# Six layer norms whose root is applied inside the transposition: a diagonal moving operand, beta as a small product, the rows in x_tok scaled a stage later

## The reference, cut to what matters

```python
def layer_norm_2(x, g, b):
    mu = jnp.mean(xf, axis=-1, keepdims=True)
    var = jnp.mean(jnp.square(xf - mu), axis=-1, keepdims=True)
    return ((xf - mu) * lax.rsqrt(var + LN_EPS) * g + b).astype(x.dtype)
...
x = layer_norm(ALPHA * x + recurrent(x), ...)        # norm 0
x = layer_norm(ALPHA * x + hier_moe(x), ...)         # norm 1
for l in range(2):                                   # second block
    x = layer_norm_2(ALPHA_2 * x + 0.5 * swiglu(x, ...), ...)   # norms 2, 5
    y = mlstm_mixer(x, ...) if l == 0 else window_attention(x, ...)
    x = layer_norm_2(ALPHA_2 * x + y, ...)                      # norms 3, 6
    x = layer_norm_2(ALPHA_2 * x + 0.5 * swiglu(x, ...), ...)   # norms 4, 7
```

## Time and profile before

| what | value |
|---|---|
| median of 3 runs | 1694.35 us (1694.08 to 1695.98) |
| the profiled execution's own time | 1697.26 us |
| its span | 1695.5 us, mean granted PE clock 0.976 |
| PE busy | 1592.3 us (94%), x9238 |
| DVE busy | 779.7 us (46%) |
| ACT busy | 505.8 us (30%) |
| POOL busy | 61.4 us (4%) |

### The profile page before, as it was taken

The page is one execution under the profiler, slowest core; times in us unless marked ns, Lnnn a source line. Parts: engine busy times, 40 slices in busy tenths (PEclk is TensorE's granted clock), DMA queues, the critical chain, the costliest instruction groups (busy, mean ns, idle before and its releaser), DMA issues.

```text
span 1695.5 us, 21971 instructions
## 1 busy us (share of the span) xinstructions
PE 1592.3 (94%) x9238; PEld 1172.1 (69%) x9238; DVE 779.7 (46%) x1028; ACT 505.8 (30%) x573; POOL 61.4 (4%) x104
## 2 busy tenths in 40 slices
PE   8997899999999998999998899999999997899997
PEld 7744433333333336999896689998999986689997
DVE  1584411111111116544656675456544566564445
ACT  1251100000000003334354234342443435433432
POOL 2000000000000000000000000000000000000000
PEclk9997899999999999999999999999999998999999
DMA  6705799999999999753223578554554221387500
GB/s 198 250 1 232 290 415 429 428 429 429 428 428 429 429 412 353 268 183 114 75 78 122 174 243 292 185 185 161 202 190 157 98 76 74 100 288 264 193 0 26
DMA packets 149457, 395.27 MB, mean 233 GB/s; under 512 B 9442, under 2 KB 109920, under 8 KB 136592
## 3 DMA queue, kind: packets, MB, share of 16 engines
q1 hardware_dynamic: 146656, 385.67, 60.5%
q0 software_dynamic: 2736, 8.68, 1.4%
HBM read 393.28 MB, written 1.05 MB: 233 GB/s over the span
## 4 chain that ended last, share of the span: by engine, by line
PE 67%; DMA 14%; DVE 10%; issue 3%; SPq 3%; ACT 2%; POOL 1%; POOLq 0%; DVEq 0%; ACTq 0%
PE bank L1355 29%; DMA ring<-in_moe_w_dram 14%; PE bank L1368 12%; PE bank L885 8%; PE bank L914 2%; PE bank L697 2%; SPq L267 2%; PE bank L1343 2%; PE bank L1575 1%; PE bank L902 1%; PE bank L644 1%; PE bank L1900 1%; PE bank L934 1%; DVE stats L539 1%; PE bank L683 1%
## 5 line engine op out<-in xcount | busy, mean ns | idle before, releaser
L885 PE MATMUL bank<-ring,arena 128*64 128x512 f32 x928 | 228.4, 596 | 9.5 <-DMA ring<-in_moe_w_dram 9.5
L1355 PE MATMUL bank<-x_hi,split_u_hi 128*128 128x256 f32 x688 | 194.9, 283 | 0.0
L1355 PE MATMUL bank<-x_hi,split_u_lo 128*128 128x256 f32 x688 | 194.7, 283 | 0.0
L1355 PE MATMUL bank<-x_lo,split_u_hi 128*128 128x256 f32 x688 | 194.7, 283 | 0.0
L1355 PE MATMUL bank<-x_lo,split_g_hi 128*128 128x256 f32 x656 | 185.6, 283 | 0.0
L1355 PE MATMUL bank<-x_hi,split_g_lo 128*128 128x256 f32 x656 | 185.6, 283 | 0.0
L1355 PE MATMUL bank<-x_hi,split_g_hi 128*128 128x256 f32 x656 | 185.6, 283 | 0.0
L885 PEld LDWEIGHTS bank<-ring,arena 128*64 128x64 f32 x928 | 69.3, 137 | 146.3 <-issue 114.7
L1265 DVE TENSOR_TENSOR split_g_lo<-ring,split_g_hi 128x2048 fp32r<-128x2048 f32 x47 | 107.7, 2292 | 127.7 <-ACT split_g_hi L1259 127.7
L1115 DVE SCALAR_TENSOR_TENSOR arena<-arena,work 128x256 f32<-128x256 f32 x32 | 15.5, 485 | 287.7 <-PE bank L934 287.7
L1265 DVE TENSOR_TENSOR split_u_lo<-ring,split_u_hi 128x2048 fp32r<-128x2048 f32 x45 | 103.1, 2292 | 69.0 <-ACT split_u_hi L1259 69.0
(11 more groups left out here) (352 smaller groups left out, 2504.8 us busy)
## 6 DMA issues: line engine op xcount, KB each, us to landing
ring<-in_moe_w_dram SPq DMA_DIRECT2D x92, 2048.0 KB, 19.1
ring<-in_ffn_w_in_dram SPq DMA_DIRECT2D x88, 1024.0 KB, 5.5
ring<-in_ffn_w_out_dram SPq DMA_DIRECT2D x44, 1024.0 KB, 5.5
ring<-in_ml_w_in_dram SPq DMA_DIRECT2D x12, 1024.0 KB, 5.2
ring<-in_rec_w_in_dram SPq DMA_DIRECT2D x10, 1024.0 KB, 11.6
ring<-in_at_w_in_dram SPq DMA_DIRECT2D x6, 1024.0 KB, 5.2
ring<-in_rec_w_out_dram SPq DMA_DIRECT2D x5, 1024.0 KB, 13.6
gb_row<-in_ln_g_dram POOLq DMA_DIRECT2D x8, 512.0 KB, 7.3
```

Source lines behind the costliest of these rows:

```text
L885: i = nc.tensor.matmul(bank[4 + p][64 * j:64 * j + 64, :], xe[p][:, k, :], unit_view(n, 4)[:, k % 4, :], start=(k == 0), stop=(k == KT - 1))
L1355: i = nc.tensor.matmul(up_bank(kind, s_)[:, m * T:(m + 1) * T], w, xp_[b][:, k, :], start=(k == 0 and j == 0), stop=(k == KT - 1 and j == 2))
```

## The change

In norms 1 to 6 the root no longer has to be in `x_tok` before PE starts. ACT builds `turn_diag`, the unit matrix times `rstd` on its rows; PE multiplies the centred tile with it, which transposes and scales at once. Beta comes into the same bank as a product ahead of it: `beta_r` (36 rows: the eight pieces of beta rounded, in rows 0 to 3, and the rest, in rows 32 to 35) with `blocks_r`, a constant matrix of ones in four blocks. `x_tok` itself is scaled later, in `finish_rows`, which the next stage calls. The rest of the diff merges the semaphores of the two attention-like stages (`ml["s"]`, `at["s"]` and others become `hd["s"]`, with counts moved by MLH) and places new tensors over dead ones; that is left out here.

```diff
+        def finish_rows(dve, L):
+            for t in range(TT):
+                for hf in range(2):
+                    dve.wait_ge(G["ln_tr"], 4 * L + 2 * t + hf + 1)
+                    scaled_rows(dve, L, t, hf)
...
         def norm_pool(pool, L):
...
+            if L in SPLIT_NORMS:
+                parts = bs.rearrange("o (b k p) -> (o k) b p", b=2, p=P)
+                pool.wait_ge(G["ln_blo"], 2)
+                for row in (0, 32):
+                    pool.dma_start(beta[row:row + 4], parts).then_inc(s_gbrow, 16)
...
         def norm_dve(dve, own, L, alpha):
...
+            if L in SPLIT_NORMS:
+                dve.wait_ge(s_gbrow, rows_loaded(L))
+                dve.wait_ge(G["ln_bhi"], SPLIT_NORMS.index(L) + 1)
+                nc.vector.tensor_tensor(beta_r[32:36], beta[32:36], beta_r[32:36].bitcast(F32), ALU.subtract).then_inc(G["ln_blo"], 1)
+                for t in range(TT):
+                    residual(t, 0)
+                    residual(t, 1)
+                    moments(t)
+                    centred(t, 0)
+                    centred(t, 1)
...
         def norm_evac_act(act, L):
+            if L in SPLIT_NORMS:
+                act.wait_ge(s_gbrow, rows_loaded(L))
+                act.wait_ge(G["ln_tr"], 4 * L)
+                nc.scalar.activation(beta_r[:], beta[:], ACT.Copy).then_inc(G["ln_bhi"], 1)
             for t in range(TT):
+                if L in SPLIT_NORMS:
+                    act.wait_ge(G["ln_rstd"], 2 * L + t + 1)
+                    nc.scalar.activation(turn_diag[:, t, :], ident[:], ACT.Copy, scale=rstd[:, t:t + 1]).then_inc(G["ln_diag"], 1)
...
         def norm_pe(pe, L):
             for t in range(TT):
                 keep_warm(pe, WARM[t])
+                n = SPLIT_NORMS.index(L) if L in SPLIT_NORMS else None
+                if n is not None:
+                    pe.wait_ge(G["ln_blo"], n + 3)
+                    pe.wait_ge(G["ln_cen"], 4 * n + 2 * t + 1)
+                    for b in range(2):
+                        nc.tensor.matmul(bank[4 + 2 * t + b][:], beta_r[:, b, :], blocks_r[:], start=True, stop=False,
+                                         skip_group_check=True)
+                    pe.wait_ge(G["ln_diag"], 2 * n + t + 1)
...
+                        i = nc.tensor.matmul(o, x_tok[:, t, k * P:(k + 1) * P], turn_diag[:, t, :], start=False, stop=(k % 4 == 3),
+                                             skip_group_check=True)
...
         moe_dve, ahead of expert 0:
+            own.did(nc.vector.memset(beta[:], 0.0))
+            own.then(nc.vector.tensor_scalar(rows, wide, 0.0, None, ALU.mult))
+            for row in (0, 32):
+                nc.vector.tensor_tensor(rows[row:row + 4], wide[0:4], ident[0:4, 0:4].unsqueeze(2).broadcast_to((4, 4, P)),
+                                        ALU.mult).then_inc(G["ln_blo"], 1)
...
         ffn_dve:
+                if s_ == 0:
+                    finish_rows(dve, NORM_AHEAD[f])
```

More of the change, by code:

```diff
@@ L127, in build @@
         ident = sb("ident", [P, P])
+        small_at = nc.sbuf_base
+        MS = sb("ml_small", [P, 256])
+        raw_at = nc.sbuf_base
+        misc_raw = sb("misc_raw", [8 * CH, P])
+        ng_raw = sb("ng_raw", [KT, P])
+        beta = nc.alloc_sbuf_tensor_at("beta", [36, 2, P], F32, offset=raw_at)
+        iota_at = nc.sbuf_base
+        iota_s = sb("iota_s", [P, SLOTS])
+        blocks_r = nc.alloc_sbuf_tensor_at("blocks_r", [36, HALF], F32R, offset=iota_at)
         upper = sb("upper", [P, P])
@@ L171, in build @@
         G = {}
-        for name in ("ln_in", "ln_var", "ln_rstd", "ln_half", "ln_tr", "ln_evac", "ln_lo"):
+        for name in ("ln_in", "ln_var", "ln_rstd", "ln_half", "ln_tr", "ln_evac", "ln_lo", "ln_cen", "ln_diag",
+                     "ln_bhi", "ln_blo"):
             G[name] = sem(name)
@@ L516, in pool_program, with rows_loaded @@
                     at_pool(pool)
+        def rows_loaded(L):
+            return 32 * (L + 1) + 32 * len([n for n in SPLIT_NORMS if n <= L])
         def norm_pool(pool, L):
@@ L558, in norm_dve @@
             if L > 0:
                 dve.wait_ge(G["ln_half"], 4 * L)
[L560 to L573, removed]
+            if L in SPLIT_NORMS:
[8 more added lines that the diff above has]
+                    centred(t, 1)
+            else:
+                residual(0, 0)
+                residual(0, 1)
+                moments(0)
+                dve.wait_ge(s_gbrow, rows_loaded(L))
+                centred(0, 0)
+                centred(0, 1)
+                scaled(0, 0)
+                scaled(0, 1)
+                residual(1, 0)
+                residual(1, 1)
+                moments(1)
+                for hf in range(2):
+                    centred(1, hf)
+                    scaled(1, hf)
@@ L1102, in moe_dve @@
             nc.vector.memset(h_e[0:64, :], 0.0).then_inc(mo["h0"], 1)
+            rows = blocks_r[:].rearrange("q (k j) -> q k j", k=4)
+            wide = ones[0:36, :].unsqueeze(1).broadcast_to((36, 4, P))
+            own.did(nc.vector.memset(beta[:], 0.0))
[3 more added lines that the diff above has]
+                                        ALU.mult).then_inc(G["ln_blo"], 1)
             for b in range(BLOCKS):
@@ L1641, in turned_weights @@
             def turned_weights(h):
[L1642 to L1643 removed]
+                act.wait_ge(hd["tr"], h + 1)
+                nc.scalar.activation(p_T[h % 2], bank[H_BANK[h]][:].rearrange("p (s j) -> p s j", s=TT), ACT.Copy).then_inc(hd["pt"], 1)
             def output_high(h):
```

111 lines of the change are left out of this document (60 added, 51 removed).

## The result

The changed kernel takes 1700.36 us (median of 9 runs, 1696.66 to 1701.69), the kernel before 1694.35 (9 runs, 1693.61 to 1696.33). The ratio is 1.0032, with a 95% interval of 1.0022 to 1.0042: it is slower, by more than the 0.2% that can be told. The forecast was 1692.1, with a range up to 1695.5.

A forecast was written before the change was run, and what follows sets the result against it. The prediction took norms to cost what PE loses between stages, waiting for DVE. Norms 2 to 6 (-0.4), norm 6's clock (-1.1) and norm 1 (-0.7) gave -2.2 us, from 1694.35 to 1692.1; range 1689.5 to 1695.5.

The forecast's parts named there:

- PE's own work is the bound of norms 2 to 6: Norms 2 to 6: the second diagonal is ready 0.9 us before PE wants it, so PE never waits.
- T: PE's first start in a norm, from which the forecast counted when the other engines' results are ready.
- Its sum, 6.3 us: PE's work per norm: beta 0.46 twice, diagonals 1.79 twice, warm products 1.79; norms 2 to 6 change by -0.4 us.
- that they have 36 rows instead of 128 should change nothing: Beta's products in each norm: priced like 512-column short-format products at 0.228 us, so 0.46 a pair.
- The clock no longer falls in norm 6: Norm 6: PE no longer waits, so the fall to the low clock level goes, saving 1.1 us.
- In norms 2 to 5, where PE waits less long: Reason given for norm 6's gain: with shorter waits in these norms the next products ran at full pace, 5.74 us.
- Norm 1: First norm: DVE waits 1.5 us for beta, yet -0.7 us in all; bounds -2.5 and +3.8.
- rise at 654.0: Norm 1: PE's clock falls at about 650.4, rises at 654.0 and doesn't fall a second time.
- 665.0: Norm 1: end of the next stage's 48 products in the kernel before, against 664.3 forecast for the changed one.
- What is hidden: Scalings (3.0 us of DVE), expert-stage DVE instructions (2.1 us) and beta's preparation in norms 2 to 6 lie under waits.
- Rival A: Low clock in norm 1 vanishes early, other stages' stretches move: -1.8 and -0.8 us more, 1689.5; chance 0.19.
- C: Diagonal products dearer than warm ones, +1.8 us a norm, 1702.9; decided by a fill from 7.3 us; chance 0.08.

The follow-up runs named there:

- beta_first: The changed kernel with all four beta products of a norm side by side ahead of token tile 0's diagonal products: 1699.79 us, ratio 1.0025.
- before_again: The kernel before executed once more with nothing edited, as a control: 1696.09 us, ratio 1.0002.
- nw_late: The changed kernel without warm products and with DVE's subtraction for beta behind the moments of token tile 0: 1690.34 us, ratio 0.9976.
- scale_tiny: The changed kernel with the later scaling of x_tok working on 8 columns of each half instead of 512: 1700.28 us, ratio 1.0029.
- the second pair: Profiled executions of the kernel before and the changed kernel, each run once more with nothing edited: 6.25 us apart.
- beta_none: The changed kernel with the four small beta products of each norm left out: 1693.06 us, ratio 0.9992.
- after_no_warm: The changed kernel without the sixteen records of warm products between the two token tiles of a norm: 1692.58 us, ratio 0.9991.
- combo1: The changed kernel without warm products, with the late subtraction and the four beta products side by side: 1694.24 us, ratio 0.9996.
- beta_none_nw: The changed kernel with neither warm products nor beta products: 1694.3 us, ratio 0.9995.

## Why the prediction was wrong, step by step

1. **PE's own work is the bound of norms 2 to 6: right.** No idle time, the second diagonal ready 3.6 us behind T, the evacuations not late (from its first start FFN 1 needs 5.99 us for 48 products, before 5.98).
2. **Its sum, 6.3 us: mis-sized, the main error.** Measured 6.93 (7.02 ahead of an FFN). The step that failed is "that they have 36 rows instead of 128 should change nothing", with a pair of beta products at 0.46. Each pair costs 0.85: its own 0.46, and 0.39 around it, 0.1 each ahead of it, between its two, ahead of the first diagonal record and behind that one (beta_first, and the starts of norm 3). The other prices were right: the records of the diagonals and of the warm products start 0.112 us apart. Of the two pairs' 0.78 us, 0.69 lie in the fill, and 0.09 ahead of T (0.32 from the projection's last product to beta, before 0.23). The term should have been +3.2 us and was put at -0.4.
3. **The clock no longer falls in norm 6: right,** -1.2 us for -1.1. The reason given is weaker than it sounds. "In norms 2 to 5, where PE waits less long" isn't so: ahead of the last transpositions PE waited 1.77 and 0.80 us in norm 4 and 1.64 and 0.79 in norm 6, and only in norm 6 did the clock fall (the first of each pair):

```profile
1186.36 0.66 PE L616 MATMUL bank<-ident,x_tok 128*128 128x128 f32 x4 [1.77 <-DVE x_tok L555]
...
1495.75 0.66 PE L616 MATMUL bank<-ident,x_tok 128*128 128x128 f32 x4 [1.64 <-DVE x_tok L555]
```

Without a wait the clock stayed up in all five norms of the changed kernel; what singled out norm 6 before stays open.

4. **Norm 1: wrong sign,** +1.6 for -0.7, inside its bounds, and +2.8 against the second execution of the kernel before. The wait for beta was right (residual 1.6 us late, PE's start 5.41 us behind the last expert product, before 5.17). What failed is "rise at 654.0": the clock was low for 6.8 us, not 3.6, and the warm products took 2.83 us, not the 1.8 given to them. The beta terms are short here too (1.12 for 0.46, and 0.66). The end that the forecast compared with, 665.0, holds the kernel before's second fall of the clock, which before_again doesn't have. The length of the low stretch follows neither from the wait nor from the start (see nw_late), and its cause stays open.
5. **What is hidden: right.** The scalings (scale_tiny; DVE's wait in attention has shrunk from 4.57 to 2.00 us), the expert stage (its last product starts at 643.2 and 643.8 us, before at 644.7 and 643.5), beta's copies in norms 2 to 6.
6. **Not in the sum: the mLSTM and attention stages,** +0.3 and +0.85. Rival A had seen that falls of the clock "move with the work", but only as a gain. They are the same in a second execution and other in other kernels with the same code. Attention's is PE's work at the low level, 2.0 us more of it; why the clock falls where it does stays open.

The sum of these (1.6 + 0.4 + 3.2 - 1.2 + 0.3 + 0.85) is the 5.2 us of the profiled executions; the medians differ by 6.0 and the second pair by 6.25. Of the rivals C came nearest in time, but its mechanism isn't there: the diagonal product is no dearer than the warm one (32 records a norm at 0.112), and the fill stays below the 7.3 us that were to decide for it. For the exchange itself, eight transpositions (0.87 us) for eight diagonal products (1.79), the traces give 1.8 us a norm, which I had by the rows; by the factor of four in "Terms" of the Trainium skill's page "TensorE: Matmul & The Clock Gate" I had 2.7. The trace stays with the factor of two.

## What to carry to other kernels

When a change fills an engine's wait with work, look for what stood in that wait as a filler: here eight warm products, worth 9.5 us before, cost 7.8 us after. Then the bound moves again, and it can be a queue's order (ACT's diagonal behind an evacuation) rather than any duration. Price an instruction by rows in which it has the shape and the neighbours that it will have: products of 36 rows between products of 128 cost nearly twice their own pace. And take the pace of a row from single starts, not from the distance between its first record and the next group's, which takes in what happens at the edges.

## What was unexpected of the hardware

- A group of products with 36 rows between products with 128 costs PE 0.39 us more than its pace, whether it has two or four. That it is the rows is argued by exclusion. Going from the short format to float32 at 128 rows costs nothing (0.23 us to the first diagonal in beta_none).
- With the same code in it, a stage with waits differs by up to 2.3 us between kernels, with the place of the low stretches of the clock; FFN 1 and FFN 2, where PE doesn't wait, stay within 0.15 us in all versions with their clock up (188.10 to 188.25).
- The same wait can leave the clock up or not. In the new form of the norm waits of PE of 0.2 to 1.2 us left it up in norms 2 to 6 (after_no_warm, combo1); a wait of 1.86 us left it up in four norms and not in the fifth (beta_none_nw). Two executions of the kernel before differ in whether it falls a second time behind norm 1.
